# Head norms rooted over a quarter of the columns, and the first modulation matrix's latent parts summed on VectorE

## What is computed

```
mod   = (silu(c) @ w_ada + b_ada).reshape(B, 6, 1, D)      # latent
mod_c = (silu(c_ctx) @ w_ada + b_ada).reshape(6, 1, 1, D)  # context
p_l = modulate(x, norm1_g, mod[:, 0], mod[:, 1]) @ w_in
p_c = modulate(ctx, norm1_g, mod_c[0], mod_c[1]) @ w_in
q, k = rms_norm(pq over heads of 64, qn_g), rms_norm(pk over heads of 64, kn_g)
att = rms_norm(o over heads of 128, subln_g) * (1 - lam_init)
kk  = k * k_k;  kk = kk / max(sqrt(sum(kk*kk over heads of 64)), 1e-12)
x   = x + mod[:, 2] * merged;  then mod[:, 3..5] around the experts
```

## Time and profile before

| | us |
|---|---|
| median of three runs | 2243.79 |
| lowest and highest | 2242.5, 2245.96 |
| the profiled execution | 2247.81 |
| its span in the profile | 2246.0 |
| first product of the projections | 36.30 |
| first product of round 0 | 125.45 |
| first product of the attention | 241.40 |
| barrier before the recurrence passed | 377.64 |

### The profile page before, as it was taken

The page is one execution under the profiler, slowest core; times in us unless marked ns, Lnnn a source line. Parts: engine busy times, 40 slices in busy tenths (PEclk is TensorE's granted clock), DMA queues, the critical chain, the costliest instruction groups (busy, mean ns, idle before and its releaser), DMA issues.

```text
span 2246.0 us, 39238 instructions
## 1 busy us (share of the span) xinstructions
PE 2149.9 (96%) x16042; PEld 1505.5 (67%) x16042; DVE 1141.6 (51%) x2438; ACT 468.7 (21%) x1062; POOL 0.2 (0%) x4
## 2 busy tenths in 40 slices
PE   7999998999989999999999999989999999999998
PEld 4554476998874333333344677478888887779998
DVE  4047797544333222121233557177777763647785
ACT  3010442544121000000011147120110001541110
POOL 0000000000000000000000000000000000000000
PEclk8999998999999999999999999999999999999999
DMA  9264755000655999999981220223345343123442
GB/s 393 81 235 177 268 200 226 4 4 4 257 211 203 417 422 422 422 422 422 422 367 38 75 75 2 75 75 150 129 171 206 113 188 131 57 76 132 169 169 76
DMA packets 59908, 431.67 MB, mean 192 GB/s; under 512 B 6640, under 2 KB 6896, under 8 KB 8048
## 3 DMA queue, kind: packets, MB, share of 16 engines
q1 hardware_dynamic: 57600, 416.31, 47.2%
q10 hardware_dynamic: 2160, 13.22, 1.5%
HBM read 428.45 MB, written 1.05 MB: 191 GB/s over the span
## 4 chain that ended last, share of the span: by engine, by line
PE 81%; DMA 9%; DVE 8%; ACT 1%; issue 1%; SPq 0%; ACTq 0%; DVEq 0%
PE bank L657 78%; DMA arena<-in_w 8%; PE bank L836 1%; DVE bank L2067 1%; DMA ring<-in_w 1%; DVE arena L2088 1%; DVE normed L2023 0%; DMA arena<-in_xin 0%; DVE arena L2289 0%; PE bank L1143 0%; PE bank L1157 0%; DVE arena L2294 0%; DVE small L2063 0%; DVE arena L2330 0%; PE bank L1380 0%
## 5 line engine op out<-in xcount | busy, mean ns | idle before, releaser
L657 PE MATMUL bank<-arena 64*64 64x64 f32 (+9 forms) x8950 | 871.0, 299 | 21.4 <-DMA arena<-in_w 6.2
L657 PEld LDWEIGHTS bank<-arena 64*64 64x64 f32 (+4 forms) x8950 | 625.4, 153 | 234.3 <-issue 184.2
L657 PE MATMUL bank<-normed,ring 128*128 128x256 f32 (+3 forms) x1984 | 512.5, 417 | 10.7 <-DVE normed L2042 5.5
L657 PEld LDWEIGHTS bank<-normed,ring 128*128 128x128 f32 (+1 forms) x1984 | 354.5, 195 | 156.7 <-issue 115.8
L657 PE MATMUL bank<-ring,arena 128*64 128x512 f32 (+1 forms) x1000 | 208.9, 604 | 13.9 <-DMA ring<-in_w 12.3
L657 PE MATMUL bank<-arena,ring 128*128 128x256 f32 (+1 forms) x1136 | 214.8, 339 | 4.1 <-DVE arena L2816 3.6
L657 PEld LDWEIGHTS bank<-arena,ring 128*128 128x128 f32 x1136 | 184.2, 191 | 22.7 <-DVE arena L2816 4.2
L657 PEld LDWEIGHTS bank<-ring,arena 128*64 128x64 f32 (+1 forms) x1000 | 62.3, 132 | 148.8 <-issue 113.5
L2578 DVE TENSOR_TENSOR arena<-arena,bank 128x512 f32<-128x512 f32 x68 | 46.6, 685 | 131.0 <-PE bank L657 129.0
L1929 ACT ACTIVATE arena<-arena 128x256 f32<-128x256 f32 (+1 forms) x88 | 32.0, 364 | 344.0 <-DVE arena L2813 217.2
L657 PE MATMUL bank<-normed,arena 128*128 128x256 f32 (+2 forms) x424 | 83.6, 340 | 0.0
(11 more groups left out here) (401 smaller groups left out, 1772.3 us busy)
## 6 DMA issues: line engine op xcount, KB each, us to landing
ring<-in_w SPq DMA_DIRECT2D x297, 1024.0 KB, 6.9
arena<-in_w SPq DMA_DIRECT2D x97, 1024.0 KB, 17.3
arena<-in_xin ACTq DMA_DIRECT2D x3, 1024.0 KB, 6.2
arena<-in_nab ACTq DMA_DIRECT2D x1, 2048.0 KB, 8.6
con<-in_con ACTq DMA_DIRECT2D x1, 1280.5 KB, 13.6
sw<-in_sw ACTq DMA_DIRECT2D x1, 1280.0 KB, 8.8
sw<-in_sw ACTq DMA_DIRECT2D x1, 1168.0 KB, 19.6
sw<-in_w SPq DMA_DIRECT2D x1, 1024.0 KB, 12.5
```

The lines of the kernel that those rows point to most:

```text
L657: return nc.tensor.matmul(o, l, r, start=start, stop=stop, **kw)
```

## The change

- `IN_ROUND` becomes 0: the rounds hold no modulation tiles. The two slabs of the first matrix behind its first one (outputs 16 to 47, in blocks of 128) are packed by output, two outputs a tile, and their 16 tiles are put among the 8 weight tiles of the projections, behind the first three (`PROJ_MODS`); TensorE skips them, VectorE sums each with two multiply-and-sums (`early_modulations`) against silu(c) as a row on every partition (`early_row`, a load of 0.5 MB and a Silu on ScalarE). SP waits for VectorE's count before it loads into such a slot. The second block's matrix keeps its 24 tiles on TensorE: 16 in `STEPS`, 8 in `LEFT`. Only latent parts are summed; the context's stay zero.
- Head norms: `head_sums` puts the four quarters of the columns in four strips of 32 partitions, root and inverse run over a quarter, `head_spread` spreads them in eight matmuls over half the array each. TensorE waits for the inverse (`qk_inverse`, `kk_inverse`) before it spreads. All four unit keys are now finished in rounds 4 to 7. In a round the order on TensorE is: sums, product 2x, spread, (keys' sums), product 2x + 1, permutation, (keys' spread). On VectorE: inverse, shift(2x), gain, shift(2x + 1), (keys' inverse), rotation, (unit keys).
- After the attention: one bank of sums for four heads, one root, one inverse, spreads in two banks behind the four modulation tiles; the gain is multiplied in with the result.

```diff
@@ -150,7 +150,7 @@
 ADA = N_ADA // UPT
-MODS = 2 * ADA
+MODS = KD + ADA
@@ -171,6 +171,9 @@
+EARLY_MODS = [(o, 0) for o in range(OUTS_BOTH, OUTS)]
+PROJ_MODS = {KD + at: j for at, j in zip((3, 5, 6, 7, 9, 10, 11, 13, 14, 15, 18, 19, 20, 21, 22, 23), range(len(EARLY_MODS) // 2))}
+
 NORMS = ("n1", "n2", "n3", "n4", "n5", "n6")
@@ -179,7 +182,7 @@
-IN_ROUND = 2
+IN_ROUND = 0
 WITH_DIFF, WITH_NORM, WITH_LORA = (0, 1, 1, 1, 1, 1, 1, 1, 1, 1, 1), (1, 1, 1, 1), (1, 0, 0, 0, 1, 0, 0, 0)
...
@@ -631,6 +635,9 @@
+                while st["ring"] is ring_full and st["unit"] % UPT == 0 and st["unit"] // UPT in PROJ_MODS:
+                    st["unit"] += UPT
+                    st["free"].append(None)
                 u = st["unit"]
...
@@ -1001,6 +1008,25 @@
+            def head_sums(src, n):
+
+                j = job("act")
+                for g in range(4):
+                    last = mm(banks[j[0]][32 * g:32 * g + 32, 0:n // 4], blk[:, 48:80], src[:, g * n // 4:(g + 1) * n // 4],
+                              True, True)
+                done(j, last)
+                return gave["act"]
+
+            def head_spread(src, n):
+
+                j = job("dve")
+                for g in range(4):
+                    for hh, h in enumerate(HALVES):
+                        row = 32 * g + 16 * hh
+                        last = mm(banks[j[0]][h, g * n // 4:(g + 1) * n // 4], ident[:, row:row + 1].broadcast_to((P, 64)),
+                                  src[:, 0:n // 4], True, True)
+                done(j, last)
+
             def rwkv_tile(m):
@@ -1013,26 +1039,24 @@
                 pe.wait_ge(S("qk_sq"), x + 1)
-                j = job("act")
-                last = mm(banks[j[0]][:, 0:n], blk, qk_sq[:, x % 2, 0:n], True, True)
-                done(j, last)
-                rooted.append(gave["act"])
+                rooted.append(head_sums(qk_sq[:, x % 2, :], n))
                 for g in round_tiles(x):
...
                 rwkv_tile(2 * x)
+                pe.wait_ge(S("qk_inverse"), x + 1)
+                head_spread(rs2[:, x % 2, :], n)
+                if x >= 4:
+                    pe.wait_ge(S("kk_sq"), x - 3)
+                    keys_rooted.append(head_sums(e1 if x % 2 == 0 else e2, T))
+                rwkv_tile(2 * x + 1)
                 pe.wait_ge(S("qk_normed"), x + 1)
...
                 if x >= 4:
-                    jt = x - 4
-                    pe.wait_ge(S("kk_sq"), jt + 1)
-                    j = job("act")
-                    last = mm(banks[j[0]][:, :], blk, e1 if jt % 2 == 0 else e2, True, True)
-                    done(j, last)
-                    keys_rooted.append(gave["act"])
-                rwkv_tile(2 * x + 1)
+                    pe.wait_ge(S("kk_inverse"), x - 3)
+                    head_spread(e3 if x % 2 == 0 else e4, T)
             pe.wait_ge(S("rotated"), 8)
@@ -1042,15 +1066,22 @@
-            marks["diffnorm"] = {}
+            j = job("act")
             for h in range(4):
-                marks["diffnorm"][h] = dict(gave)
                 pe.wait_ge(S("diff_sq"), h + 1)
-                j = job("act")
-                last = mm(banks[j[0]][:, 0:SEQ], ones, w1b[:, h, :], True, True)
-                done(j, last)
+                last = mm(banks[j[0]][32 * h:32 * h + 32, 0:SEQ], ones[:, 0:32], w1b[:, h, :], True, True)
+            done(j, last)
+            marks["heads_rooted"] = gave["act"]
             for h in range(4):
                 second_slab(AT_NORM + h)
+            pe.wait_ge(S("head_inverse"), 1)
+            for pair_of in range(2):
+                j = job("dve")
+                for x in range(2):
+                    h = 2 * pair_of + x
+                    last = mm(banks[j[0]][:, x * SEQ:(x + 1) * SEQ], ident[:, 32 * h:32 * h + 1].broadcast_to((P, P)),
+                              dstd[:, 0, :], True, True)
+                done(j, last)
@@ -1704,11 +1735,14 @@
             modulation(KD - 1)
+            act.dma_start(early_row, dram["crow1"]).then_inc(S("early_row_in"), 16)
             act.dma_start(region(16640, 1280), dram["cnt"]).then_inc(S("counts_in"), 16)
...
             modulate("n1", slice(0, T), mod1[:, 0:16])
+            act.wait_ge(S("early_row_in"), 16)
+            f(early_row, early_row, ACT.Silu).then_inc(S("early_row_silu"), 1)
             copies(4, lambda j: pool_in[:, j, :])
@@ -1721,6 +1755,7 @@
                 b = a.take()
+                n //= 4
                 a.gives(f(rs2[:, x % 2, 0:n], b[:, 0:n], ACT.Sqrt, bias=eps_c[:, 2:3] if x < 4 else eps_c[:, 0:1],
@@ -1730,7 +1765,7 @@
                     b = a.take()
-                    a.given(f(e3 if jt % 2 == 0 else e4, b[:, :], ACT.Sqrt))
+                    a.given(f((e3 if jt % 2 == 0 else e4)[:, 0:P], b[:, 0:P], ACT.Sqrt))
@@ -1751,9 +1786,8 @@
                 a.signals(f(w1b[:, h, :], w1a[:, h, :], ACT.Square), "diff_sq")
-            for h in range(4):
-                b = a.take()
-                a.given(f(dstd[:, h, :], b[:, 0:SEQ], ACT.Sqrt, bias=eps_c[:, 0:1], scale=1.0 / P))
+            b = a.take()
+            a.given(f(dstd[:, 0, :], b[:, 0:SEQ], ACT.Sqrt, bias=eps_c[:, 0:1], scale=1.0 / P))
             act.wait_ge(S("shifted"), 1)
...
@@ -2108,6 +2143,18 @@
+            def early_modulations(lo, hi):
+
+                dve.wait_ge(S("early_row_silu"), 1)
+                for i in range(lo, hi):
+                    o, x = EARLY_MODS[i]
+                    t = min(t for t in PROJ_MODS if PROJ_MODS[t] == i // 2)
+                    dve.wait_ge(ring_full[t % RING], 16 * (t // RING + 1))
+                    w = ring[:, t % RING * TILE + i % 2 * D:t % RING * TILE + (i % 2 + 1) * D]
+                    V.tensor_tensor_reduce(out=w, in0=w, in1=early_row, scale=1.0, scalar=Q("b_ada", 2 * o), op0=MUL,
+                                           op1=ADD, accum_out=mod1[:, 2 * o:2 * o + 1]).then_inc(S("early_modulated"), 1)
+
+            early_modulations(0, 8)
             dve.wait_ge(S("tables_in"), 16)
@@ -2129,9 +2176,11 @@
                 v.signals(tt(w1a[:, g, :], w1a[:, g, :], pool_in[:, g, :], SUB), "pool_diff")
+            early_modulations(8, 28)
             for g in range(4):
...
                 v.given(ts(pool_out[:, g, :], b[:, 0:SEQ], Q("pool_scale", g), None, MUL))
+            early_modulations(28, len(EARLY_MODS))
@@ -2147,13 +2196,19 @@
+            def keys_inverse(jt):
+
+                dve.wait_ge(back["act"], marks["keys_rooted"][jt])
+                r = (e3 if jt % 2 == 0 else e4)[:, 0:P]
+                v.does(ts(r, r, 1e-12, None, MAX))
+                v.signals(V.reciprocal(r, r), "kk_inverse")
+
             def unit_keys(jt):
-                dve.wait_ge(back["act"], marks["keys_rooted"][jt])
-                r = e3 if jt % 2 == 0 else e4
-                v.does(ts(r, r, 1e-12, None, MAX))
-                v.does(V.reciprocal(r, r))
-                v.signals(tt(KK[:, jt, :], KK[:, jt, :], r, MUL), "kk_unit")
+                b = v.take()
+                v.given(tt(KK[:, jt, :], KK[:, jt, :], b[:, :], MUL))
+                dve.wait_ge(back["dve"], v.n_back)
+                dve.nop().then_inc(S("kk_unit"), 1)
@@ -2177,24 +2232,29 @@
                 lat = q_in[:, x, :] if x < 4 else k_in[:, x - 4, LAT]
-                r = rs2[:, x % 2, 0:n]
+                r = rs2[:, x % 2, 0:n // 4]
                 dve.wait_ge(back["act"], marks["qk_rooted"][x])
-                v.does(V.reciprocal(r, r))
-                v.signals(stt(out=src, in0=src, scalar=Q("q_norm_g" if x < 4 else "k_norm_g"), in1=r,
-                              op0=MUL, op1=MUL), "qk_normed")
+                v.signals(V.reciprocal(r, r), "qk_inverse")
                 for g in round_tiles(x):
...
                 shift(2 * x)
+                b = v.take()
+                v.gives(stt(out=src, in0=src, scalar=Q("q_norm_g" if x < 4 else "k_norm_g"), in1=b[:, 0:n],
+                            op0=MUL, op1=MUL))
+                dve.nop().then_inc(S("qk_normed"), 1)
+                if 2 * x + 1 < NRW:
+                    shift(2 * x + 1)
+                if x >= 4:
+                    keys_inverse(x - 4)
                 rotate(lat, C("cos64"), C("sin64"), pads[2][:, 0:SEQ], "rotated")
-                if x in (5, 6):
-                    unit_keys(x - 5)
+                if x >= 4:
+                    unit_keys(x - 4)
                 if x == 6:
                     keys_squared(3)
-                if 2 * x + 1 < NRW:
-                    shift(2 * x + 1)
+            dve.wait_ge(S("early_modulated"), len(EARLY_MODS))
             v.does(ts(mod1[:, 32:48], mod1[:, 32:48], 0.5, None, MUL))
...
@@ -2230,14 +2291,23 @@
             v.signals(V.memset(small[:, LM + 5:LM + 6], 0.0), "diff_evac")
+            dve.wait_ge(back["act"], marks["heads_rooted"])
+            v.signals(V.reciprocal(dstd[:, 0, :], dstd[:, 0, :]), "head_inverse")
             for h in range(4):
-                dve.wait_ge(back["act"], marks["diffnorm"][h]["act"] + 1)
```

(50 more changed lines are left out.)

## The result

The changed kernel takes 2260.89 us (median of 6 runs, 2257.41 to 2261.52), the kernel before 2243.65 in the same comparison: a ratio of 1.0074, 95% interval 1.0061 to 1.0087. The change makes the kernel 17.2 us slower, where 8.6 were forecast.

What follows compares the result with a forecast made beforehand. The rounds were taken as TensorE-bound. Terms 8.2 - 5.3 + 6.2 - 2.3 + 4.8 - 3.0 gave +8.6 on the profiled 2247.81 us, 2256, which stood 4.0 above the median: forecast 2252 us, range 2243 to 2260.

Steps and rivals of the forecast that it cites:

- the ring: Projections: the six-slot weight ring keeps up, the values' weights landing with 1.5 us to spare; cost 0.
- rival 2: End of rounds 4 to 6: the keys' inverse isn't waited for; 14.3 us less, 2238.1 us; chance 0.08.
- rival 4: Start of the rounds: the first weight tile isn't late; 9.7 us less, 2242.7 us; chance 0.06.
- first tile late: Start of the rounds: first weight tile lands at 131.2 us, TensorE waits, clock costs 2.0; round 0 ends 8.2 us later.
- rounds 1 to 3: Rounds 1 to 3: products, rotations, sums and spreads take 37.8 us instead of 43.1; -5.3 us.
- rounds 4 to 6, without clock: Rounds 4 to 6: 60.4 us instead of 54.2, with three waits for the keys' inverse, 10.8 us together; +6.2 us.
- round 7, without clock: Round 7: ends with VectorE's shift, gain, keys' inverse and rotation, 8.8 us instead of 11.15; -2.3 us.
- clock behind the key waits: Rounds 4 to 6: each of three waits for the keys' inverse loses 1.6 us to half clock; +4.8 us, bounds 0 and 9.
- attention: Attention: one transpose group less, but VectorE's softmax sets the pace and hides the saving; 0, if not a few tenths.
- after the attention: After the attention: fewer roots and inverses, LoRA products start 1 us sooner, clock stays up; -3.0 us (-1 to -5).
- rival 1: Rounds 4 to 6: the clock holds through the waits for the keys' inverse; +3.8 us, 2247.6 us; chance 0.22.
- rival 3: Projections: the values' weights come 2 to 5 us late; with clock loss some 5 us more, 2257.5 us; chance 0.12.

Runs made afterwards that it cites:

- the run with filled waits: The changed kernel with seven unread 128x256 matmuls ahead of each of the three waits for the keys' inverse; 2253.21 us.
- the run with the filled attention: The kernel with both added waits removed, plus four unread 128x128 products in the attention where the removed transposes stood; 2235.87 us against 2236.45.

## Why the prediction was wrong

The mechanism was right: the two waits were there, at their places and from their causes, the ring held in the projections, and what rival 2 and rival 4 priced for their absence was measured as 13.7 us (14.3 in rival 2) and 11.8 (9.7 in rival 4). What failed is the size: 17.2 instead of 8.6. The step that failed is the pricing of the sum's terms: the products and small groups of rounds 1 to 6, too low by 3.1 us together, the attention, put at 0 (1.6), the late first tile (1.5) and the clock behind the key waits (1.4). The traces up to the barrier say so term by term; they are one execution of each kernel. A round is taken from the start of its sum to that of the next; where the sum is merged with a permutation or a keys' spread, that one's 0.43 or 1.06 us is taken off.

| term | forecast | measured | missed by |
|---|---|---|---|
| first tile late | +8.2 | +9.7 | 1.5 |
| rounds 1 to 3 | -5.3 | -3.7 | 1.6 |
| rounds 4 to 6, without clock | +6.2 | +7.7 | 1.5 |
| round 7, without clock | -2.3 | -1.9 | 0.4 |
| clock behind the key waits | +4.8 | +6.2 | 1.4 |
| attention | 0 | +1.6 | 1.6 |
| after the attention | -3.0 | -2.8 | 0.2 |
| sum at the barrier | +8.6 | +16.8 | 8.2 |

No term was far off; all seven missed to the same side.

**First tile late.** "it lands at 121.5 + 4.7 + 2 x 2.5 = 131.2": TensorE started on it at 132.37, 1.2 us later. Of these 0.4 are there at the values already (94.29 against 93.88), the rest came with the landing; the other 0.3 lie in round 0's products and groups. The clock's 2.0 was right: 5.66 against 3.72.

**Rounds 1 to 3 and 4 to 6.** Here the prediction argued with the wrong kind of number, "every matmul being two instructions" times a mean duration. The mean says what an instruction in a long row of its like costs, not what a group costs that interrupts another. From start to start a spread of 64 columns is 0.61 us (174.60 - 173.99), with 0.5 counted; permutation and sum are 0.77 (166.92 - 166.15), with 0.63 counted; and the product behind a small group takes 7.07 or 6.97 (173.99 - 166.92, 181.57 - 174.60) and not 6.87 (in the kernel before, too, a product behind modulations took 6.97: 145.10 to 152.07 us). A long round is 15.42 us (181.57 - 166.15) and not 14.87: 0.55 a round. In rounds 4 to 6 products are over the forecast again (6.97 us from 190.82 to 197.79 in the run with the keys' inverse first), while a long spread with its sum was as counted (1.38 us from 189.52 to 190.90, with 1.4 counted); and each key wait is 3.82 us from the end of the product (201.69 - 197.87), not 3.6.

**The clock.** Forecast at three times 1.6. Measured by the lengthened rows: 9.03 - 7.13 and 2.56 - 1.45 behind the first wait, 1.11 and 0.34 behind the second, 5.41 - 3.72 behind the third: 6.2 us, within the bounds of 0 and 9. The Trainium skill ("TensorE: Matmul & The Clock Gate", section "Why this matters for your kernels") advises against idle gaps between bursts, as TensorE drops to half rate after one. By that rule every key wait costs its clock; the run with filled waits agrees (7.7 us back). Other runs agree only in part, see the last section.

**Attention.** "0, if not a few tenths": it took 34.9 us (294.28 - 259.38) and before 33.3 (from 241.40 to 274.69). The products behind the idle of 1.79 us ran at 1.2 GHz for a while (0.79 over 264 to 272): rows of 1.75 and 2.08 us at 265.82 and 267.49, where the same groups take 1.06 and 1.13 at 270.99 and 271.98, that is 1.6. Removed work left a hole, and the hole cost clock in the changed kernel. In the kernel without the two waits, and in those without one of them, the same hole cost nothing: the attention took 33.4 us in all of them. What decides between the two was not settled.

**After the attention** the forecast stood as a number, and in its cause for the greater part: the gap ahead of the LoRA products is gone, and the granted clock is 1.00 over 296 to 314 us where the kernel before had 0.91. But counted from the head sums the LoRA products start 0.35 us sooner and not 1 (301.83 - 294.28 against 282.59 - 274.69), since the spreads of 1.99 us now stand ahead of them; they are through 1.9 us sooner (313.12 and 295.46), and where the rest up to the barrier was won was not looked into. The run with the heads' norm alone gives it 4.0 us by the medians.

**The rivals.** None came: the clock fell (against rival 1), the keys' inverse was waited for (2), no load was late for the values (3), and the first tile of the rounds was late (4). The result lies 0.9 us above the range of 2243 to 2260: its upper end was built from one more wait, rival 3, and took in no common error of the other terms.

## What to carry to other kernels

Before a change is judged, ask of each wait that it adds whether the waiting engine's work or only the releasing engine's order of instructions causes it: here two VectorE steps in the wrong order cost 13.7 us and the first tile of the rounds, loaded behind two tiles that only VectorE reads, 11.8, while the change itself was worth 7.6. Time each part alone as well: the modulation part with its tile early paid 7.9 us and the norm after the attention some 4, and the new norms in the rounds paid nothing. And price a small group on a busy TensorE from start to start, with what the next product loses. The errors of a sum's terms need not cancel: here all seven had one sign, and the range should allow for that.

## What the runs showed of the hardware

The clock does not answer equal idles equally. The idle of 3.23 us with the same instructions around it came three times in the kernel with the tile early. Busy time by stretch there, one stretch for each:

```profile
190.00:207.00 17.00, 16.05 (x75) 8.13 (x76) 10.39 (x16) 1.27 (x3) 0.00 (x0) 0.90 0.32 123
210.00:225.00 15.00, 11.86 (x69) 6.03 (x70) 10.03 (x16) 1.27 (x3) 0.00 (x0) 1.00 0.19 71
225.00:240.00 15.00, 11.77 (x78) 7.26 (x76) 8.48 (x14) 0.37 (x1) 0.00 (x0) 1.00 0.19 70
```

The first cost clock, the other two did not; in the changed kernel all three did. Two idles of 1.3 and 0.55 us at about 180 us left the clock at 0.86 over 178 to 190 in the modulation part with its tile early, and at 1.00 in the kernel that adds the heads' norm to it, which has the same work and the same two idles up to there (first row the one without the heads' norm, second row the one with it):

```profile
178.00:190.00 12.00, 10.94 (x22) 4.78 (x23) 5.60 (x10) 1.23 (x2) 0.00 (x0) 0.86 0.04 16
```

```profile
178.00:190.00 12.00, 10.24 (x24) 4.58 (x25) 7.22 (x12) 1.82 (x3) 0.00 (x0) 1.00 0.14 52
```

Nor are long idles needed: the attention's first row was at the lower clock behind idles of 1.15, 0.61 and 0.28 us (3.46 us, with the key waits filled), and at the full one behind idles of 0.95, 0.60 and 0.28 us in the kernel without the two waits (2.00 us).

So the clock's price for such an idle is between nothing and some 3 us, and it can differ between executions of one kernel: the one with only its tile early had runs from 2243.24 to 2255.7 us, with a mean granted clock of 0.984 in the fastest and 0.978 in the slowest, while the one with filled key waits kept within 1.3 us. That gaps always bring such a spread is not shown: the head-norm part alone, with its three key waits, kept within 2.9 us, and the run with the filled attention spread by 5.9. But the profile of a kernel with gaps is one draw, and its clock losses should be read as such.
